# Keeping four instead of eight of the first layer's shift tiles for the context's columns

## The reference

```python
sc = jax.nn.silu(c)
scc = jax.nn.silu(c_ctx)
mod = sc @ ada_w[layer] + ada_b[layer]
shift, scale, gate = jnp.split(mod[:, None, :], 3, axis=-1)
h = modulate(rmsnorm(x, norm_g[layer]), shift, scale)
mod_c = (scc @ ada_w[layer][:, :n_mod] + ada_b[layer][:n_mod])[None, None, :]
hc = modulate(rmsnorm(xc, norm_g[layer]), mod_c[..., :D_MODEL], mod_c[..., D_MODEL:2 * D_MODEL])
k, v, q, za, glu, zb = jnp.split(h @ w_in, EV_SPLITS, axis=-1)
kc, vc = jnp.split(hc @ w_in[:, :2 * KV_W], 2, axis=-1)
```

## Time and profile before

| | |
|---|---|
| Runs shown | median 3104.55 us of 3 (3099.26 to 11257.15) |
| Profiled execution, its own time | 3101.12 us |
| Its span in the trace | 3099.3 us |
| PE busy, share of the span | 2755.9 us, 89% |
| DVE busy, share of the span | 2040.1 us, 66% |
| Loads of `aring` from `ada` | 200 of 1 MiB |
| DMA over the whole span | 943.04 MB, mean 304 GB/s |

### The profile page before, as it was taken

The page is one execution under the profiler, slowest core; times in us unless marked ns, Lnnn a source line. Parts: engine busy times, 40 slices in busy tenths (PEclk is TensorE's granted clock), DMA queues, the critical chain, the costliest instruction groups (busy, mean ns, idle before and its releaser), DMA issues.

```text
span 3099.3 us, 32106 instructions
## 1 busy us (share of the span) xinstructions
PE 2755.9 (89%) x12484; PEld 2333.5 (75%) x12484; DVE 2040.1 (66%) x2773; ACT 614.0 (20%) x1264; POOL 911.1 (29%) x716
## 2 busy tenths in 40 slices
PE   5899889999999999899999999767677766999997
PEld 4778668788888788777888888766576655666664
DVE  8889565737535437712564227999999979656666
ACT  1012240110010110012100011122257777000000
POOL 1100001101000000000010003677677666656664
PEclk9999999999999999998999999888787776999998
DMA  9984368949877633231698448999999997999998
GB/s 355 373 351 138 136 234 322 391 164 373 351 276 298 272 111 108 107 122 69 269 421 339 149 147 355 417 421 421 419 417 421 409 391 226 399 413 413 414 414 343
DMA packets 148160, 943.04 MB, mean 304 GB/s; under 512 B 16449, under 2 KB 16449, under 8 KB 50753
## 3 DMA queue, kind: packets, MB, share of 16 engines
q0 software_dynamic: 102528, 612.41, 49.0%
q1 hardware_dynamic: 44352, 320.65, 26.9%
q10 hardware_dynamic: 1152, 8.26, 0.7%
HBM read 937.06 MB, written 4.19 MB: 304 GB/s over the span
## 4 chain that ended last, share of the span: by engine, by line
PE 65%; DVE 14%; DMA 8%; ACT 7%; issue 4%; POOL 3%; DVEq 0%; SPq 0%; ACTq 0%
PE G L460 41%; PE M L951 14%; DMA aring<-ada 3%; DVE proj L1670 3%; DMA vec<-peer_u,proj 3%; ACT vec L1258 2%; PE M L910 2%; DVE aring L1395 2%; DVE vec L2044 2%; POOL aring L434 1%; DVE proj L1477 1%; PE G L898 1%; ACT vec L1263 1%; ACT vec L1266 1%; POOL ring L434 1%
## 5 line engine op out<-in xcount | busy, mean ns | idle before, releaser
L460 PE MATMUL G<-h,ring 128*128 128x256 f32 x4864 | 1075.8, 384 | 14.1 <-ACT h L997 14.1
L460 PEld LDWEIGHTS G<-h,ring 128*128 128x128 f32 x4864 | 935.4, 193 | 144.4 <-issue 17.2
L419 POOL DMA_DIRECT2D aring<-ada x200 | 105.7, 529 | 1578.0 <-DVE mods L1395 1561.1
L1395 DVE CUSTOM_DVE_ANT_0 aring<-aring,acc,vec 128x2048 f32<-128x2048 f32 x168 | 391.2, 2350 | 135.7 <-DMA aring<-ada 134.3
L460 PE MATMUL G<-proj,ring 128*128 128x256 f32 x2080 | 456.4, 383 | 0.9 <-DVE proj L1891 0.9
L460 PEld LDWEIGHTS G<-proj,ring 128*128 128x128 f32 x2080 | 399.3, 192 | 55.9 <-issue 2.0
L434 POOL DMA_INDIRECT aring<-peer_u,proj x130 | 240.4, 1850 | 325.2 <-DVE proj L1978 190.5
L951 PE MATMUL M<-sq,mix 128*128 128x512 f32 x688 | 299.1, 593 | 0.7 <-ACT mix L1272 0.7
L951 PEld LDWEIGHTS M<-sq,mix 128*128 128x128 f32 x688 | 204.5, 297 | 91.3 <-ACT mix L1272 0.9
L2016 DVE CUSTOM_DVE_ANT_0 aring<-sq,aring 128x2048 f32<-128x2048 f32 x104 | 236.6, 2291 | 31.9 <-DMA aring<-peer_u,proj 21.2
L962 ACT ACTIVATE proj<-G 128x256 f32<-128x256 f32 (+1 forms) x168 | 64.3, 383 | 973.7 <-PE G L460 973.6
(11 more groups left out here) (349 smaller groups left out, 2872.3 us busy)
## 6 DMA issues: line engine op xcount, KB each, us to landing
ring<-weights SPq DMA_DIRECT2D x217, 1024.0 KB, 5.0
aring<-ada POOLq DMA_DIRECT2D x200, 1024.0 KB, 12.1
sq<-v_blocks SPq DMA_DIRECT2D x43, 1024.0 KB, 8.0
proj<-v_blocks SPq DMA_DIRECT2D x21, 1024.0 KB, 8.0
ring<-first SPq DMA_DIRECT2D x16, 1024.0 KB, 7.1
acc<-v_rows,proj POOLq DMA_INDIRECT x151, 9.2
aring<-peer_u,proj POOLq DMA_INDIRECT x130, 13.0
acc<-conds ACTq DMA_DIRECT2D x2, 1024.0 KB, 7.2
```

The costliest lines, as they stand in the source:

```text
L419: pool.dma_start(aring[:, n % SLOTS, :], ada[a]).then_inc(ada_in[n % SLOTS], 16)
L460: mm = nc.tensor.matmul(bank[:, 0:TOK], lhsT=ring[:, slot, weights_at + t * P:weights_at + (t + 1) * P], rhs=rhs[:, t, :], start=(t == ord ...
L1395: V_.tensor_tensor_reduce(out=tile, in0=tile, in1=vector, scale=1.0, scalar=bias, op0=ALU.mult, op1=ALU.add, accum_out=column).then_inc(ad ...
```

## The change

One constant goes from 8 to 4, and with it `ADA0` from 40 to 44.

```diff
-KEPT = 8
+KEPT = 4
 ADA0 = 32 + DT - KEPT
```

## The result

| | before | changed |
|---|---|---|
| Median of 16 runs each | 3105.18 us | 3113.01 us |
| Profiled execution, its own time | 3101.12 us | 3110.21 us |
| Its span | 3099.3 us | 3108.3 us |
| Loads of `aring` from `ada` | 200 | 204 |
| DMA over the whole span | 943.04 MB | 947.24 MB |

The ratio is 1.0024, with a 95% interval of 1.0016 to 1.0032: 7.5 us slower, between 5.0 and 9.9. The forecast said 7 us slower and no difference by 2%. DVE is busy for the same time (2040.3 us, 2040.1 before).

A forecast was written before the change was run, and what follows sets the result against it. It took DVE to bound rounds 4 to 7, transfers the rounds' end and the remaining shift columns, then DVE through the keys' squares. 3101.12 - 7.5 + 14.0 + 0.5 = 3108.1 us; range 3098 to 3118.

The forecast's parts named there:

- The rounds, -7.5: First load: four rounds lose one context product each on DVE, so the rounds end 7.5 us earlier, at about 163.5.
- the forecast's two limits, 5.8 and 9.1: Gain in the rounds: 5.8 us if only transfer shares rise to 0.99, at most 9.1 us by DVE's four products.
- the forecast's 377 to 394 and 408: Transfers in the rounds: 377 and 394 GB/s if only shares rise to 0.99; 408 GB/s is the next stretch's rate.
- Rival B: In the rounds, 343 GB/s is what the queues give, so the rounds do not get shorter; 3115.6 us, chance 0.14.
- The second load, +14.0: After the context's squares: four more tiles loaded and reduced start the reciprocal 14.0 us later, counted from the rounds' end.
- the last load that was read in the kernel before: Second load: last of the four next tiles, issued at 208.0, lands at 220.4; its product ends at 222.75.
- PE's restart, +0.5: First `head_sum`: after nearly 14 us idle, restart costs PE 2.6 us, 2.15 us of it spare, leaving 0.5 (0 to 2).
- the 3106 to 3112 given for it: Whole kernel: forecast time with the scatter of the earlier runs, 3.4 us above to 1.9 below the profiled execution.
- 3104 to 3113 by the ends of its terms: Whole kernel: span claimed for the forecast from its terms' ends, given chance 0.63.
- A: Second load is hidden, tiles coming as fast as DVE takes them; reciprocal 7.5 us earlier, 3093.6 us, chance 0.07.
- C: Rounds gain 9.1 us and the four tiles cost 9.2 at 2.57 us each; 3101.7 us, no difference, chance 0.12.
- No later stage waits for something that keeps its own time: After the rotation: everything follows from the same chain, so the 7 us reach the end.

The follow-up runs named there:

- loads alone: Kernel before, eight shift tiles kept in the rounds, but twelve tiles loaded again, four columns made twice; median 3118.84 us, ratio 1.0032.
- sum early: PE's sum and ACT's root put after two of four units: on the kernel before 3103.59 us (0.9989), on the changed kernel 3112.24 us (1.0022).
- rounds alone: Changed kernel's rounds, but only eight tiles loaded again; context shift columns of tiles 4 to 7 left out; median 3101.23 us, ratio 0.9979.
- other load later: Changed kernel with the third conditioning row, 1 MiB, loaded only beside the convolution; median 3112.08 us, ratio 1.0018.
- products between the squares: Two products ahead of the context's squares, two between their halves: on the changed kernel 3108.24 us (1.0016), on the kernel before 3103.86 us (0.9989).
- kernel 7: Kernel before with ten shift tiles kept, six loaded again, and PE's sum with ACT's root after two of four units; median 3104.94 us, ratio 0.9993.

## Why the prediction was right

**The rounds, -7.5.** They ended 7.24 us earlier in the profiled pair, and 5.5 us over the means of all traces with 8 and 4. The pair lies between the forecast's two limits, 5.8 and 9.1; the means lie just below the lower one, so the closeness of 7.24 to 7.5 is partly luck. The mechanism was right: round 4 has no wait, the first is at 88.17, and the mean rate, 397 GB/s, lies between the forecast's 377 to 394 and 408. Rival B (the rate of 343 GB/s can't be passed) is out.

**The second load, +14.0.** It was +11.0 in the changed kernel and +14.2 with the loads alone. The step that mis-sized it for the changed kernel is the last load that was read in the kernel before: its landing was counted from the end of the rounds as if all waits ahead of it stayed as they were. Split by the waits in the brackets, the first eight products of the changed kernel wait 5.8 us for tiles and those of the kernel before 8.5; the four more take 9.1 us of work and wait 5.5; the root's 1.1 is gone. That is -2.7 + 9.1 + 5.5 - 1.1 = 10.8, and the readouts' small gaps make up the rest of the 11.0. The first eight waited 8.3 (loads alone) and 6.7 us (sum early) with `KEPT = 8`, and 5.3 (rounds alone), 6.4 (sum early) and 5.8 us (other load later) with `KEPT = 4`: less in every one with `KEPT = 4`, though the groups nearly touch, and with `KEPT = 6` it was 9.8. So it may be the shorter rounds or the scatter of the transfers, which stays open; the loads are issued at the same distances from the end of the rounds in both traces (the pairs at 164.01 and 171.43 before, at 156.75 and 164.19 changed).

**PE's restart, +0.5.** In the profiled pair this was too small, and its mechanism was looked for at the wrong sum. The idle time of 10.75 us at the first (14 expected, less by the 3 us of the step above) made the first products 1.6 us longer, which the slack took. But the second sum, after an idle of 2.11 us like that of before (1.90), ran 1.67 us longer, and L577 1.4 us longer. The two add some 2.7 to 3 us to the path. That size is no fixed price of the change: in the three other kernels with four tiles kept and twelve loads the second sum kept its 1.89 us after idle times of 2.41, 2.28 and 1.71 us, and what PE added up to the first attention's end was 1.1, 1.4 and -0.1 us. The forecast's 0 to 2 us fits these three, and the 2.7 of the pair lies above.

**The sum.** So the +7.0 came out as -7.24 + 11.0 + 2.7 = 6.5 us at 608 and 1122 us, and as 7.5 us in the timing: right in total, with two terms off by 3.0 and 2.2 us in opposite directions, which is luck. The forecast of 3108 stands on the profiled execution of before, 3101.12, which is 4 us below that kernel's median; the profiled execution of the changed kernel took 3110.21, and the median, 3113.01, lies above the 3106 to 3112 given for it. "3104 to 3113 by the ends of its terms" doesn't follow from the terms as written: their ends (5.8 to 9.1, 9.2 to 19.5, 0 to 2) give 3101 to 3117. The reciprocal was forecast at 215.2 and came at 212.52; the second sum at 330.8, it came at 327.57. The rank of the causes is shown: take the four loads and their products away and the time after the rounds is 1.2 us under before, keep the four products and take only their loads away, and 10 of the 11.0 us are gone; move the root alone in the changed kernel, and nothing changes.

**The rivals.** A and C have their reciprocal before 209, the trace at 212.52; A's hidden load is out, as the waits for `ada` say, and of C the part of the four tiles that land faster is half true: they took (210.25 - 195.33) / 4 = 3.73 us each, between 2.57 and the 4.03 of the earlier trace rows.

**The stages after.** "No later stage waits for something that keeps its own time" holds from 608 to 1122 us, where the delay stays at 6.5 us. Between the second sum and 608 it doesn't: a gain of 7.3 us became 4.2, 4.7 became 2.2 and 3.5 became 1.6, and a delay of 3.8 became 6.5. PE at its lower clock took those, as the table of all kernels shows.

## What to carry to other kernels

When a step is moved away from an engine-bound stretch into one where its data must come again, compare the two limits of each stretch, not the work: here 9.1 us of products were worth 5.5 to 7 us where they left, cost 2.2 us where they arrived, and their 4 MiB cost 10 more. Read the time of added transfers from how the same ring goes on in the trace of before, and give the waits ahead of them 2 to 3 us of scatter. Where two arms end within 1 us of each other, as the tiles and the root did, shortening one gives little more than their distance, and lengthening one costs in full: products between the squares gave 0.0 us after the rounds, four more loads cost 14.2.

## What the runs showed of the hardware

- After a short idle time the same group of products can run at either level of PE's clock. The eight products of the second sum took 1.89 us after 0, 1.53, 1.71, 1.87, 1.90, 2.28 and 2.41 us of waiting, and 3.25, 3.56, 2.67 and 3.31 us after 2.04, 2.11, 3.59 and 5.23 us. Four products at L577, always after 2.39 or 2.40 us, took 1.95 or 1.96 us in five kernels (granted clock 1.00 in the kernel before) and 3.03 to 3.75 us in nine (0.50 in kernel 7). So the length of the wait alone doesn't decide it, and two profiles can differ by 1.0 to 4.5 us at the first attention's end for this alone.
- The transfers to one core went at 421 GB/s for 32.8 us, from memory into two rings at once, more than the 408 that the kernel before had shown.
- Kernels whose first load is the same code can differ by 5.6 us at its end (169.12 to 174.72), while each of DVE's products there takes 2.34 or 2.35 us.
